# Modulation vectors of a transformer block: sixteen of 24 weight chunks multiplied and added by VectorE instead of TensorE

## The reference, cut to what matters

```
def adaln_params(cond, w_mod, b_mod):
    m = jax.nn.silu(cond) @ w_mod + b_mod          # w_mod: 1024 x 6144
    return jnp.split(m, 6, axis=-1)

sh1, sc1, g1, sh2, sc2, g2     = adaln_params(c, w_mod, b_mod)
csh1, csc1, cg1, csh2, csc2, _ = adaln_params(c_ctx, w_mod, b_mod)
hc = rmsnorm(xc, n1) * (1 + csc1) + csh1           # of the context only k and v are used
h  = rmsnorm(x, n1) * (1 + sc1) + sh1
q, k, v, gb, gcv, u, ga, gv = split_proj(h @ w_in)
x  = x + g1 * merge_branches(windowed_attention(...) @ w_attn_out, conv_branch(...), ga, gv, w_mix_out)
h2 = rmsnorm(x, n2) * (1 + sc2) + sh2
x  = x + g2 * peer(h2, ...)                        # per token 128 rows of a table are gathered
```

## Time and profile before

| | us |
|---|---|
| median of three runs | 1722.07 |
| lowest, highest | 1720.96, 1734.61 |
| the profiled execution | 1734.19 |
| its span, first to last instruction | 1732.4 |
| PE busy | 1535.8 (89%) |
| DVE busy | 1038.3 (60%) |
| ACT busy | 769.7 (44%) |
| POOL busy | 272.4 (16%) |
| mean granted clock of TensorE | 0.950 of full |
| read from memory | 429.62 MB, 249 GB/s over the span |

### The profile page before, as it was taken

The page is one execution under the profiler, slowest core; times in us unless marked ns, Lnnn a source line. Parts: engine busy times, 40 slices in busy tenths (PEclk is TensorE's granted clock), DMA queues, the critical chain, the costliest instruction groups (busy, mean ns, idle before and its releaser), DMA issues.

```text
span 1732.4 us, 22946 instructions
## 1 busy us (share of the span) xinstructions
PE 1535.8 (89%) x8428; PEld 1125.5 (65%) x8428; DVE 1038.3 (60%) x2079; ACT 769.7 (44%) x1648; POOL 272.4 (16%) x260
## 2 busy tenths in 40 slices
PE   7899998969988898887878879898999987899997
PEld 3799657845444333332323249788999986899997
DVE  1345326376666666776666447535777766467774
ACT  2444334224444444444444353545555545455553
POOL 0000000044433444444444300000000000000000
PEclk9699999989999999999999999879999998899997
DMA  7154444399999999999999934304555431244551
GB/s 289 68 195 171 170 146 146 122 377 423 427 427 427 426 427 427 426 428 426 427 427 427 428 147 146 122 1 160 181 173 190 169 122 49 73 163 178 187 176 73
DMA packets 59986, 431.76 MB, mean 249 GB/s; under 512 B 6784, under 2 KB 7296, under 8 KB 7552
## 3 DMA queue, kind: packets, MB, share of 16 engines
q0 software_dynamic: 36864, 268.45, 36.8%
q1 hardware_dynamic: 22176, 160.44, 25.7%
q10 hardware_dynamic: 864, 1.80, 0.3%
HBM read 429.62 MB, written 1.05 MB: 249 GB/s over the span
## 4 chain that ended last, share of the span: by engine, by line
PE 44%; DMA 20%; ACT 7%; DVE 6%; issue 2%; POOL 1%; ACTq 0%; POOLq 0%; DVEq 0%; SPq 0%
PE banks L594 18%; DMA arena<-in_peer_uv,experts 17%; PE banks L922 11%; PE banks L1028 7%; DMA tok_b<-in_peer_uv,experts 2%; DVE wlow L1480 2%; PE banks L809 2%; ACT diag L1300 2%; PE banks L626 1%; PE banks L783 1%; ACT scores L1208 1%; PE banks L648 1%; DVE arena L1836 1%; ACT L1292 1%; ACT L1285 1%
## 5 line engine op out<-in xcount | busy, mean ns | idle before, releaser
L922 PE MATMUL banks<-arena,diag 128*128 128x512 f32 x824 | 403.6, 626 | 95.2 <-ACT diag L1300 95.0
L922 PEld LDWEIGHTS banks<-arena,diag 128*128 128x128 f32 x824 | 150.4, 195 | 336.6 <-ACT diag L1300 200.3
L1836 DVE CUSTOM_DVE_ANT_0 arena<-arena,scores 128x1024 f32<-128x1024 f32 x206 | 252.6, 1226 | 183.8 <-DMA arena<-in_peer_uv,experts 182.8
L1480 DVE TENSOR_TENSOR wlow<-wring,whigh 128x1024 fp32r<-128x1024 f32 x234 | 275.4, 1220 | 128.9 <-ACT whigh L1071 128.8
L1442 POOL DMA_INDIRECT arena<-in_peer_uv,experts x206 | 217.4, 1055 | 650.0 <-DVE experts L1800 349.6
L1071 ACT ACTIVATE whigh<-wring 128x1024 fp32r<-128x1024 f32 x234 | 233.8, 1048 | 140.9 <-DMA wring<-in_w_qkv_a 33.4
L594 PE MATMUL banks<-f_high,whigh 128*128 128x256 f32 x720 | 205.8, 286 | 16.1 <-DVE f_low L1516 10.7
L594 PE MATMUL banks<-f_low,whigh 128*128 128x256 f32 x720 | 204.5, 284 | 0.0
L594 PE MATMUL banks<-f_high,wlow 128*128 128x256 f32 x720 | 204.4, 284 | 0.0
L1292 ACT ACTIVATE dots<-dots 128x1 f32<-128x1 f32 x256 | 51.4, 201 | 287.2 <-DVE dots L1836 286.9
L594 PE MATMUL banks<-a_high,whigh 128*128 128x256 f32 x552 | 166.1, 301 | 13.8 <-DVE a_low L1488 8.1
(11 more groups left out here) (233 smaller groups left out, 2525.1 us busy)
## 6 DMA issues: line engine op xcount, KB each, us to landing
wring<-in_w_up SPq DMA_DIRECT2D x44, 1024.0 KB, 4.8
wring<-in_w_mod SPq DMA_DIRECT2D x24, 1024.0 KB, 4.8
wring<-in_w_down SPq DMA_DIRECT2D x22, 1024.0 KB, 4.8
wring<-in_w_in SPq DMA_DIRECT2D x17, 1024.0 KB, 4.8
wring<-in_w_qkv_a SPq DMA_DIRECT2D x12, 1024.0 KB, 4.9
wring<-in_peer_w_q SPq DMA_DIRECT2D x8, 1024.0 KB, 4.9
wring<-in_w_mix_out SPq DMA_DIRECT2D x4, 1024.0 KB, 4.8
wring<-in_w_o_a SPq DMA_DIRECT2D x4, 1024.0 KB, 4.8
```

Source lines behind the costliest of these rows:

```text
L922: mm = nc.tensor.matmul(banks[:, 2 + 2 * b + half, :], diag[:, n % DIAGS, :], ring[n % RING][:, D + half * 512:D + (half + 1) * 512], star ...
L1480: V.tensor_tensor(low, w, high.bitcast(F32), ALU.subtract).then_inc(w_split, 1)
L1836: V.tensor_tensor_reduce(out=ring[n % RING][:, 0:D], in0=ring[n % RING][:, 0:D], in1=h2tok[:, b, :], scale=1.0, scalar=0.0, op0=ALU.mult, ...
```

## The change

The first eight chunks stay as they are. For the other sixteen, DVE multiplies the 128 x 256 piece of a chunk that belongs to input tile k by the column k of the condition vector c (a number per partition) and adds up the eight pieces in `mod_sum` (two buffers). PE then only sums over partitions: two products with `mod_sum` as weights and a column of ones, which leave the result as columns in bank 7, with no copy and no turn. Only c is computed in these groups, not c_ctx.

Chunks are taken in the order of `COLUMN_MODS`: g1, sc2, sh2, g2. The first twelve (n = 0 to 11) leave SP's ring: POOL loads them in two halves of 0.5 MB each into `mod_half`, the last 8 KB per partition of the arena, one buffer per half, from the time that seven of the first chunks are used. DVE does column n after a split: columns 0 to 4 after the splits of w_in chunks 5 to 9, 5 and 6 after 11 and 12, 7 to 9 after 13 to 15, 10 and 11 in turns 2 and 5 of the attention. PE sums column n behind projection tile n+6, and columns 10 and 11 in turns 4 and 7. The last four come through SP's ring as before; DVE adds one of their pieces in each of the rows 88 to 119, and PE sums after rows 98, 106, 114 and 122.

```
+COLUMN_MODS = [8, 9, 10, 11, 16, 17, 18, 19, 12, 13, 14, 15, 20, 21, 22, 23]
+MODS_MIX, MODS_NORM = 4, 12
+        mod_sum = sb("mod_sum", [P, 2, WIDE])
+        mod_half = arena[:, 56 * T:64 * T].rearrange("p (h k n) -> p h k n", h=2, n=WIDE)
...
-        add_mods(MODS_1, MODS_2)
...
-        add_mods(MODS_2, MOD_TILES // 2)
+        gate_chunks = [add(chunk_of(a["w_mod"], COLUMN_MODS[n]), (column_added, n + 1), split=False)
+                       for n in range(MODS_NORM, len(COLUMN_MODS))]
...
+            def mod_columns(n):
+                pe.wait_ge(column_added, n + 1)
+                for j in range(2):
+                    t = 2 * COLUMN_MODS[n] + j
+                    mm = nc.tensor.matmul(banks[:, 7, 2 * t:2 * t + 1], mod_sum[:, n % 2, j * P:(j + 1) * P], ones[:, 0:1],
+                                          start=True, stop=True)
+                mm.then_inc(column_made, 1)
...
                 mm.then_inc(proj_made, 1)
+                if i >= 6:
+                    mod_columns(i - 6)
...
-                    if which == 0:
-                        mod_chunk(MODS_1 + i)
+                    if which == 0 and i in (4, 7):
+                        mod_columns(10 + (i == 7))
...
-                if n in MOD_ROWS:
-                    mod_chunk(MODS_2 + MOD_ROWS.index(n))
+                if n - 10 in MOD_ROWS:
+                    mod_columns(MODS_NORM + MOD_ROWS.index(n - 10))
...
-                    if which == 0:
-                        rows_out(MODS_1 + i)
...
-                if n - 1 in MOD_ROWS:
-                    rows_out(MODS_2 + MOD_ROWS.index(n - 1))
...
+            pool.wait_ge(mod_rows, MODS_1 - 1)
+            for n in range(MODS_NORM):
+                i = COLUMN_MODS[n]
+                for part in range(2):
+                    if n > 0:
+                        pool.wait_ge(half_added[part], n)
+                    pool.dma_start(mod_half[:, part, :, :].rearrange("p k n -> p (k n)"),
+                                   a["w_mod"][i * P:(i + 1) * P, part * CHUNK // 2:(part + 1) * CHUNK // 2]
+                                   ).then_inc(half_in[part], 16)
...
+            def add_rows(n, k, w):
+                total = mod_sum[:, n % 2, :]
+                step.settle()
+                if k == 0:
+                    if n >= 2:
+                        dve.wait_ge(column_made, n - 1)
+                    return V.tensor_scalar(total, w, csil[:, k, 0:1], None, ALU.mult)
+                return V.scalar_tensor_tensor(out=total, in0=w, scalar=csil[:, k, 0:1], in1=total, op0=ALU.mult,
+                                              op1=ALU.add)
+            def column_mod(n):
+                for part in range(2):
+                    dve.wait_ge(half_in[part], 16 * (n + 1))
+                    for k in range(KT // 2):
+                        ins = add_rows(n, part * KT // 2 + k, mod_half[:, part, k, :])
...
+            for n in range(6):
                 low_next()
+                if n < 5:
+                    column_mod(n)
...
+            for n in range(2):
                 low_next()
+                column_mod(5 + n)
...
+            for n in range(4):
                 low_next()
+                if n < 3:
+                    column_mod(7 + n)
...
+                    if which == 0 and i in (2, 5):
+                        column_mod(10 + (i == 5))
...
-            dve.wait_ge(mod_made, MODS_2)
-            step.link(modulation(2 * KT, 5 * KT))
+            dve.wait_ge(column_made, MODS_NORM)
+            step.link(modulation(2 * KT, 5 * KT, 1))
...
+                    row = g * TOPK + s
+                    if MOD_ROWS[0] <= row < MOD_ROWS[0] + 8 * len(MOD_ROWS):
+                        n, k = divmod(row - MOD_ROWS[0], 8)
+                        gate_mod(MODS_NORM + n, k)
```

More of the change, by code:

```diff
@@ L45 @@
 MODS_1 = 2 * KT // 2
-MODS_2 = 5 * KT // 2
+MODS_ALL = MOD_TILES // 2
+COLUMN_MODS = [8, 9, 10, 11, 16, 17, 18, 19, 12, 13, 14, 15, 20, 21, 22, 23]
+MODS_MIX, MODS_NORM = 4, 12
 PEER_HEADS = 8
@@ L673, in mod_chunk @@
                 c = mod_chunks[i]
-                started = i not in (0, MODS_1, MODS_2)
-                if started and mod_bank(i) == mod_bank(i - 1):
-                    mod_turn(i - 1)
                 pe.wait_ge(landed[c["slot"]], c["landed"])
@@ L1518, in low_gained, with modulation @@
                     ins.then_inc(h_ready, 1)
-            def modulation(first, last):
-                bias = vcol[:, V_BMOD + first:V_BMOD + last].unsqueeze(2).to_broadcast([P, last - first, 2])
-                return V.tensor_tensor(mod[:, first:last, :],
-                                       banks[:, 7, 2 * first:2 * last].rearrange("p (t s) -> p t s", s=2), bias, ALU.add)
+            def modulation(first, last, conds):
+                bias = vcol[:, V_BMOD + first:V_BMOD + last].unsqueeze(2).to_broadcast([P, last - first, conds])
+                return V.tensor_tensor(mod[:, first:last, 0:conds], banks[:, 7, 2 * first:2 * last].rearrange(
+                    "p (t s) -> p t s", s=2)[:, :, 0:conds], bias, ALU.add)
@@ new lines, in add_rows @@
+            def add_rows(n, k, w):
[12 more added lines that the diff above has]
+                        ins = add_rows(n, part * KT // 2 + k, mod_half[:, part, k, :])
+                        if part == 1 and k == KT // 2 - 1:
+                            ins.then_inc(half_added[part], 1)
+                            dve.wait_ge(half_added[part], n + 1)
+                            dve.sem_inc(column_added, 1)
+                        elif k == KT // 2 - 1:
+                            ins.then_inc(half_added[part], 1)
+                            dve.wait_ge(half_added[part], n + 1)
+                        else:
+                            step.mark(ins)
@@ L1526, in gains, with gate_mod @@
+            def gate_mod(n, k):
+                c = gate_chunks[n - MODS_NORM]
+                if k == 0:
+                    dve.wait_ge(landed[c["slot"]], c["landed"])
+                ins = add_rows(n, k, wring[:, c["slot"], :].rearrange("p (k n) -> p k n", k=KT)[:, k, :])
+                if k == KT - 1:
+                    ins.then_inc(column_added, 1)
+                else:
+                    step.mark(ins)
             def gains(n, group, which, norm):
@@ L1537, in _ @@
             dve.wait_ge(ctx_in, 16)
-            step.link(modulation(0, 2 * KT))
+            step.link(modulation(0, 2 * KT, 2))
             dve.sem_inc(mod_ready, 1)
@@ L1564, in _ @@
                 V.tensor_tensor(pair, pair, t, ALU.add).then_inc(roped, 1)
-            for _ in range(6):
+            for n in range(6):
                 low_next()
+                if n < 5:
+                    column_mod(n)
             dve.wait_ge(proj_read, 8)
```

26 lines of the change are left out of this document (10 added, 16 removed).

## The result

The changed kernel took 1745.13 us in the median of four runs (1732.18 to 1755.07), against 1722.68 (1720.96 to 1734.61) for the kernel before in the same session: a ratio of 1.0104, 95% interval 1.0063 to 1.0144, so some 18 us slower (1.0104 less 1, times 1722). The forecast was 17.7 us less, with a range of 1692 to 1721. The prediction was wrong in sign.

The account below looks back on a forecast made before the run. PE was taken to bound projection and attention, DMA transfers the row loop. Attention 80.7 to 54 us, less 9 us of longer projection, gave 17.7 us off the 1722.1 us median: 1704.4 us, range 1692 to 1721.

Parts of the forecast that it names:

- The projection after: Projection with ten columns on DVE and ten pairs of sums on PE: 9 us longer.
- The walk has three rules: Projection: PE waits for splits, ACT rounds after evictions, DVE alternates split and column; 4.2 us longer without waiting for loads.
- 0.5 us a pair: Projection: each of PE's ten pairs of one-column sums takes 0.5 us at full clock, 5 us on PE.
- PE waiting for a column: Sign of a wrong prediction: PE waits for the columns themselves rather than for splits.
- L = 5.0: Projection: a half load lands 5.0 us after DVE frees its buffer; above 4.4 each us costs about 8 us.
- half loads late: Rival: in the projection half loads land at L = 8, costing 33 us; 1728.4 us in all; chance 0.08.
- hidden loads: Rival: in the projection loads land within 4.4 us, so it grows only 4.2 us; 1699.6 us; chance 0.24.
- walk without clock and without columns: First attention without modulation, TensorE at full clock: 46.1 us from first score to first output product, instead of 80.7.
- The clock, put at 5.5: First attention: one cold stretch and part of a second, raising 48.5 us at full clock to 54.
- both together cost 2.4 us: First attention: the two DVE columns at turns 2 and 5 add 2.4 us, giving 48.5.
- Elsewhere: Outside projection and attention: nothing gained or lost; row loop unchanged at 668 us, DVE's 14.6 us of additions there hidden.
- Wrong would be a projection longer by over 15 us: Sign of a wrong prediction: the projection grows by over 15 us, where 9 was forecast.

Follow-up runs that it names:

- One load: The changed kernel with POOL loading only the first chunk's two halves, which every column reads, two sum buffers kept: 1733.48 us, one run.
- early sums: The changed kernel, two sum buffers kept, with PE summing column n behind tile n+5 instead of n+6: 1731.16 us, ratio 1.0037 to the kernel before.
- columns ahead with two buffers: The kernel of columns ahead with two mod_sum buffers instead of four: 1710.81 us, ratio 0.9896 to the kernel before the change.
- four sums: The changed kernel with four mod_sum buffers instead of two, nothing else: 1731.16 us, ratio 1.0002 to the kernel before the change.
- both causes out: The changed kernel with four mod_sum buffers and only the first chunk's two halves loaded, read by every column: 1718.59 us, ratio 0.9951 to the kernel before.
- bare attention: The changed kernel with nothing added by DVE for columns 10 and 11 in the first attention: 1739.62 us, one run.
- deep loads: The kernel of four sums with real loads alternating between two sets of halves, the second in the score buffer: 1712.29 us, ratio 0.9886 to the kernel before.
- columns ahead: On top of deep loads, columns 0 and 1 moved into an earlier DVE gap, others two places forward, none in the attention: 1703.22 us, ratio 0.9842 to the kernel before.

## Why the prediction was wrong

**The step that failed** is in "The projection after": "The walk has three rules". It has PE waiting for splits, ACT for evictions, and DVE taking split and column in order. The change adds a fourth, a wait of DVE on PE's count of sums, which stands in the diff and was not walked. The prediction priced PE's half of this handshake (0.5 us a pair) and named PE waiting for a column as a sign of being wrong, but put the way back at nothing without a reason. Closed, it is sum, column, split, tile: 13.3 us for a tile where 6.25 was forecast, three times over, 23 us more than before. One load shows that it needs no late transfer, early sums and columns ahead with two buffers that one tile of distance opens it.

**The loads.** L = 5.0 with "8 us per us above 4.4": the median landing was 4.4 (smallest 3.5, largest 8.2), 4.7 with the 0.3 us to the issue, so the middle was about right and the spread was missing. Late halves cost 4.4 us in the change, and 14 to 19 where the ring is open (94.1 and 99.1 less 80.2 with four sums). The rival "half loads late", 1728.4 us, had the projection longer by 33 us through them alone. That 33.3 were measured is luck: in the change most of it is the ring, which waits at the same place, DVE at its columns. The rival's cause is what stood next behind the ring. The view of the line that issues them, for the change:

```profile
DMA to landing us min/median/max: 3.5/4.4/8.2
```

The Trainium skill ("DMA: Bandwidth & Descriptors", Anatomy of one DMA) gave 3.2 us, by my estimate from its figures; the smallest landing is 3.5, near it, and the median of 4.4 is above it. Its result, hidden loads at 1699.6 us, did not come. Why most halves land later than the smallest was not shown; sharing with SP's 1 MB chunks is likely, whose own median in the projection went from 4.8 to 6.0 us with four sums.

**What held of the projection.** With both causes out it is 80.2, 8.0 more than before; the walk said 4.2 without waits for loads and 9 in all. The records of a pair of sums last 0.50 us, and a tile with one takes 6.20 where it took 5.76, 0.44 more (0.5 taken). A column costs 4.00 us from its start to its last end, and 4.16 to the split behind it, where I had 3.6: the multiply-adds take 0.52 us each, not the 0.46 of the table of angles.

**The attention.** 61.95 measured, 54 forecast, inside the bounds of 48.5 and 70.4. The walk without clock and without columns, 46.1, is borne out by 47.85 at 0.92. The clock, put at 5.5 (54 less 48.5), has 6.2 left for it in the bare attention (52.3 less 46.1); this is a remainder against the walk, not a measurement, and the 7 to 15 us of slow clock that the walk took had no row behind them. The mis-sized term is "both together cost 2.4 us": the two columns brought 9.6. PE's idle time grew by 2.2, close to the 2.4 of the walk, which had every engine at its pace; the other 7.4 are products of PE that took longer at the lower clock. That the idle time lowered the clock fits the timeline, where the slow weighings stand behind idle time, but how much of the 9.6 is this stays open, as said.

**Elsewhere** the forecast held: the row loop 638.8 against 638.1, its DMA share 1.00, and the stage of the output products 83 us on either side. Two readings in the working are a little off and change nothing: 1 MB at 418 GB/s is 2.5 us, not 2.4, and DVE's 433 us over 256 rows are 1.69 us a row, not 1.65. DVE did 14.6 us more in the row loop (447.6 against 433.0) and nothing came of it. "Wrong would be a projection longer by over 15 us" is what came.

**The sum, redone.** 80.7 - 61.95 - 33.3 = -14.6. The forecast was 80.7 - 54 - 9 = +17.7. Of the 32.3 us between them 23.0 are the ring, 8.0 the attention, and 1.3 the rest of the projection (10.3 us measured, of which 5.8 are tile 12, against the 9 forecast).

## What to carry to other kernels

A buffer handed back and forth between two engines makes waits in both directions; walk both, and close the ring: what is queued behind the waiting instruction, and does the partner need that before it can release it? Count the distance in pieces of work between the release and the need. One tile is serial, two were enough here, already with two buffers. For a single-buffered load the late landings count and not the median: a second set of halves took the waits from 17.6 us to none while the loads themselves got slower. And removing the first wait in a list only shows the next one; the pair of experiments that removed both said what either alone did not.

## What the runs showed of the hardware that was not expected

- Ahead of 86 us, where the change adds only GpSimd's first two loads, the granted clock of the profiled executions was either about 0.9 or about 0.66 from 39 to 86 us, and the projection's tile 3 came 10 to 13 us earlier or later with it. That is as much as the change's own effect, and it decides which profile looks faster. What sets it is open.
- Loads of 0.5 MB issued by GpSimd landed after 3.4 or 3.5 us at least, 4.4 to 5.8 in the median and 8.2 to 10.9 at most, in the nine kernels that load all of them; the highest medians are those with two sets of halves and four sums, but the change and the bare attention, with the same code in the projection, gave 4.4 and 4.9. SP's loads of w_in went from 4.8 to 6.9 us in the median with deep loads and 6.8 with columns ahead, but only to 5.0 with the same halves and sums one tile earlier.
- By one trace of each, the same instructions of an attention took 47.85 us at a granted clock of 0.92 and 52.2 at 0.82.
